# Inverting the RWKV chunk matrices with the transposed factor in the other head's partitions, and the product copied by ScalarE

## The reference, cut to what matters

```python
def rwkv7_scan(r, decay, k, v, a_in, b_in):
    def step(state, inp):
        r_t, w_t, k_t, v_t, a_t, b_t = inp
        sa = jnp.einsum('bhvk,bhk->bhv', state, a_t)
        state = (state * w_t[:, :, None, :] + sa[..., None] * b_t[:, :, None, :]
                 + v_t[..., None] * k_t[:, :, None, :])
        y = jnp.einsum('bhvk,bhk->bhv', state, r_t)
        return state, y
```

## Time and profile before

| | us |
|---|---|
| median of three runs | 2758.38 |
| the profiled execution, its own time | 2757.62 |
| its span, first to last instruction | 2755.8 |
| PE, matmuls busy | 2643.4 |
| DVE (VectorE) busy | 1314.2 |
| ACT (ScalarE) busy | 833.2 |
| POOL (GpSimd) busy | 1038.1 |
| mean granted TensorE clock, of full speed | 0.99 |

### The profile page before, as it was taken

How to read it: one execution, slowest core, us unless ns; L and a number is a source line. 1 busy time by engine, 2 the same in 40 slices (tenths; PEclk the granted TensorE clock), 3 DMA queues, 4 the chain that set the end, 5 groups by cost and what they waited for, 6 DMA issues and landing times.

```text
span 2755.8 us, 43028 instructions
## 1 busy us (share of the span) xinstructions
PE 2643.4 (96%) x17184; PEld 2155.1 (78%) x17184; DVE 1314.2 (48%) x2476; ACT 833.2 (30%) x1687; POOL 1038.1 (38%) x1310
## 2 busy tenths in 40 slices
PE   6999999999999999998899899999999998999999
PEld 5778787877877878776688788788887887877777
DVE  4224343436847567476542533543335006477743
ACT  3344443535224131231213311211113103455531
POOL 2322332333233231320357533344445555444452
PEclk9999999999999999999999999999999999999999
DMA  3111111111101011111332211111111113111122
GB/s 130 40 40 47 50 39 50 47 43 46 44 24 58 21 47 35 37 47 51 150 122 77 84 35 42 46 40 46 46 46 46 46 46 100 35 51 39 47 108 84
DMA packets 203991, 153.94 MB, mean 56 GB/s; under 512 B 5264, under 2 KB 183824, under 8 KB 203280
## 3 DMA queue, kind: packets, MB, share of 16 engines
q1 hardware_dynamic: 186256, 106.44, 13.0%
q10 hardware_dynamic: 17536, 44.74, 4.3%
HBM read 128.10 MB, written 23.07 MB: 55 GB/s over the span
## 4 chain that ended last, share of the span: by engine, by line
PE 76%; DVE 15%; ACT 6%; POOL 2%; issue 1%; DMA 0%; DVEq 0%; ACTq 0%; SPq 0%; POOLq 0%
PE gemm L621 19%; PE gemm L623 18%; PE gemm L622 18%; ACT prob L2382 3%; DVE neg_logits L1807 2%; DVE prob L1822 2%; PE scores L672 1%; PE scores L869 1%; PE weighted L699 1%; PE probs_t L866 1%; PE probs_t L684 1%; PE scores L1046 1%; PE scores L858 1%; DVE stats L1811 1%; PE max_rows L884 1%
## 5 line engine op out<-in xcount | busy, mean ns | idle before, releaser
L582 POOL CAST w_hi<-w_raw 128x512 fp32r<-128x512 f32 x346 | 239.5, 692 | 1597.8 <-PE gemm L623 1531.4
L621 PE MATMUL gemm<-h_hi,w_hi 128*128 128x512 f32 x1904 | 779.1, 409 | 11.0 <-ACT q_t L2024 7.6
L623 PE MATMUL gemm<-h_hi,w_lo 128*128 128x512 f32 x1904 | 747.3, 392 | 0.0
L622 PE MATMUL gemm<-h_lo,w_hi 128*128 128x512 f32 x1904 | 746.1, 392 | 0.0
L584 POOL TENSOR_TENSOR w_lo<-w_raw,w_hi 128x256 fp32r<-128x256 f32 x692 | 590.0, 853 | 54.7
L621 PEld LDWEIGHTS gemm<-h_hi,w_hi 128*128 128x128 f32 x1904 | 360.3, 189 | 91.1 <-issue 22.6
L623 PEld LDWEIGHTS gemm<-h_hi,w_lo 128*128 128x128 f32 x1904 | 359.5, 189 | 78.7
L622 PEld LDWEIGHTS gemm<-h_lo,w_hi 128*128 128x128 f32 x1904 | 360.6, 189 | 66.0 <-issue 1.9
L1589 DVE TENSOR_TENSOR scaled_product<-gemm,norm_rstd 128x512 f32<-128x512 f32 x108 | 74.7, 692 | 310.9 <-PE gemm L623 308.7
L1286 DVE CUSTOM_DVE_ANT_0 neg_logits<-scores,bias_tile 128x128 f32<-128x128 f32 (+1 forms) x192 | 67.6, 352 | 148.7 <-PE scores L672 142.9
L621 PE MATMUL gemm<-xn_hi,w_hi 128*128 128x512 f32 x288 | 117.1, 407 | 4.7 <-DVE xn_lo L1735 4.3
(11 more groups left out here) (512 smaller groups left out, 4541.0 us busy)
## 6 DMA issues: line engine op xcount, KB each, us to landing
w_raw<-in_w_in SPq DMA_DIRECT2D x73, 512.0 KB, 3.9
w_raw<-in_a_w_in SPq DMA_DIRECT2D x48, 512.0 KB, 3.8
gates_scratch<-o_f ACTq DMA_DIRECT2D x32, 256.0 KB, 2.0
merge_gates<-gates_scratch ACTq DMA_DIRECT2D x4, 2048.0 KB, 14.0
w_raw<-in_a_w_out SPq DMA_DIRECT2D x16, 512.0 KB, 3.9
w_raw<-in_b_w_in SPq DMA_DIRECT2D x16, 512.0 KB, 3.8
x_rows<-in_x SPq DMA_DIRECT2D x8, 512.0 KB, 8.6
w_raw<-in_w_out SPq DMA_DIRECT2D x8, 512.0 KB, 4.0
```

The lines of the kernel that those rows point to most:

```text
L582: Q(pool.tensor_copy(weight_part(u, 0, ks), raw[:, s, ks, :]))
L621: pe.matmul(dst, w_high, hi(k, h), start=first, stop=False)
L622: pe.matmul(dst, w_high, lo(k, h), start=False, stop=False)
L623: m = pe.matmul(dst, w_low, hi(k, h), start=False, stop=last)
```

## The change

TT moves into the partitions of the other head, and Tm stays. It is now made like Tm, by TensorE: products with the identity whose input is in one head's partitions and whose output in the other's. The product X = AmT^T Tm also goes from one head's partitions to the other's, into the PSUM banks PV and MB in place of S2. Then X and TT lie side by side, TT^T X leads back to the head's own partitions and X^T TT stays in the other's, and the four products of a chunk number (two heads, two products) name four different quarters; they are issued one after the other. ScalarE copies X to SBUF in place of VectorE. VectorE adds the two halves of Tm first and signals them, then the two halves of TT. TensorE waits for the halves of Tm before X, and for those of TT only before the second products. Its waits for vr_even and vr_odd, which guard PV and MB, now stand before the levels. In AM the first of the three kinds has the heads swapped (L813, L1446, L1464), and in the scan L1507 goes by krows.

```diff
--- before.py
+++ after.py
@@ -810,7 +810,7 @@
                     for i in range(8):
                         for hh, r in enumerate(rows2):
                             c = 8 * cq + i
-                            m = pe.matmul((S2, PT2)[hh][:, i * P:i * P + P], BK[r, c, :, :], AM[r, c, 0:3:2, hh, :], start=True, stop=True)
+                            m = pe.matmul((S2, PT2)[hh][:, i * P:i * P + P], BK[r, c, :, :], AM[r, c].rearrange("p k h t -> p (k h) t")[:, 1 - hh:5 + hh:3 + 2 * hh, :], start=True, stop=True)
                     m.then_inc(E("amat_full"), 1)
 
                 products(0)
@@ -848,31 +848,34 @@
                             m = pe.matmul(PT2[r, c * C:c * C + C], AmT[r, 0, c, :], ident2[r, :], start=True, stop=True)
                     m.then_inc(E("inv_first"), 1)
                     side(p, f"inv{hf}")
+                for hf in range(2):
+                    for r, q in (rows2, rows2[::-1]):
+                        m = pe.matmul(S2[q, halves[hf]], ident2[r, :], AmT[r, 0, 8 * hf:8 * hf + 8, :], start=True, stop=True)
+                    m.then_inc(E("inv_first"), 1)
+                pe.wait_ge(E("vr_even"), 4 * p + 4)
+                pe.wait_ge(E("vr_odd"), 5 * p + 5)
                 for lv in range(1, 6):
-
+                    made = 22 * p + 4 * (lv - 1)
                     pe.wait_ge(E("a_level"), 6 * p + lv + 1)
                     for hf in range(2):
-                        pe.wait_ge(E("inv_sb"), 12 * p + 2 * lv - 1 + hf)
+                        pe.wait_ge(E("inv_sb"), made + 1 + hf)
                         for c in chunk_half[hf]:
-                            for r in rows2:
-                                m = pe.matmul(S2[r, c * C:c * C + C], AmT[r, lv % 2, c, :], Tm[r, c, :], start=True, stop=True)
+                            for r, q in (rows2, rows2[::-1]):
+                                m = pe.matmul((PV, MB)[hf][q, c % 8 * C:c % 8 * C + C], AmT[r, lv % 2, c, :], Tm[r, c, :], start=True, stop=True)
                         m.then_inc(E("invx_full"), 1)
                         side(p, f"inv{4 * lv - 2 + hf}")
                     for hf in range(2):
                         pe.wait_ge(E("invx_sb"), 10 * p + 2 * lv - 1 + hf)
-                        if lv < 5:
-                            for c in chunk_half[hf]:
-                                for r in rows2:
-                                    pe.matmul(PT2[r, c * C:c * C + C], TT[r, c, :], Xs[r, c, :], start=True, stop=True)
+                        pe.wait_ge(E("inv_sb"), made + 3 + hf)
                         for c in chunk_half[hf]:
-                            for r in rows2:
+                            for r, q in (rows2[::-1], rows2):
+                                if lv < 5:
+                                    pe.matmul(PT2[q, c * C:c * C + C], TT[r, c, :], Xs[r, c, :], start=True, stop=True)
                                 m = pe.matmul(S2[r, c * C:c * C + C], Xs[r, c, :], TT[r, c, :], start=True, stop=True)
                         m.then_inc(E("inv_full"), 1)
                         side(p, f"inv{4 * lv + hf}")
 
-                pe.wait_ge(E("vr_even"), 4 * p + 4)
-                pe.wait_ge(E("vr_odd"), 5 * p + 5)
-                pe.wait_ge(E("inv_sb"), 12 * p + 12)
+                pe.wait_ge(E("inv_sb"), 22 * p + 22)
                 for c in range(NCH):
                     n = NCH * p + c
                     pe.wait_ge(E("state"), n + 1)
@@ -1443,7 +1446,7 @@
 
                 for hh, r in enumerate(rows2):
                     V(v.tensor_tensor(AM[r, :, 2, hh, :], chunks(rT[r, :]), chunks(ec[r, :]), ALU.mult))
-                    V(v.scalar_tensor_tensor(AM[r, :, 0, hh, :], chunks(kk[r, :]), -1.0, chunks(logw[r, :]), ALU.mult, ALU.mult))
+                    V(v.scalar_tensor_tensor(AM[r, :, 0, 1 - hh, :], chunks(kk[r, :]), -1.0, chunks(logw[r, :]), ALU.mult, ALU.mult))
                     V(v.tensor_tensor(BK[r, :, hh, :], chunks(kka[r, :]), chunks(cum[r, :]), ALU.mult))
                     V(v.tensor_tensor(BK[r, :, 1 - hh, :], chunks(kmod[r, :]), chunks(cum[r, :]), ALU.mult), E("ak_ready") if hh else None)
                 if p == 0:
@@ -1461,7 +1464,7 @@
                         b, k = rows2[hh], krows[hh]
                         masked(Aab[b, cs, :], bank[b, :, 0, :], mask_a[b, 0:C])
                         masked(AM[b, cs, 1, hh, :], bank[b, :, 1, :], mask_a[b, C:2 * C])
-                        masked(AM[k, cs, 0, hh, :], bank[k, :, 0, :], mask_a[k, 0:C])
+                        masked(AM[k, cs, 0, 1 - hh, :], bank[k, :, 0, :], mask_a[k, 0:C])
                         masked(AM[k, cs, 2, hh, :], bank[k, :, 1, :], mask_a[k, C:2 * C], E("amat_done") if hh else None)
                 for f in range(4):
                     bank = (PV, MB)[f % 2][:].rearrange("p (w x c) -> p w x c", w=4, x=2)
@@ -1474,36 +1477,34 @@
                 def level_of(i):
                     V(v.tensor_tensor(AmT[:, i % 2], Aab[:], level[i].unsqueeze(1).to_broadcast([P, NCH, C]), ALU.mult), E("a_level"))
 
-                eye = ident2.unsqueeze(1).to_broadcast([P, NCH, C])
+                eye = ident2.unsqueeze(1).to_broadcast([P, 8, C])
                 level_of(0)
-                V(v.tensor_tensor(TT[:], AmT[:, 0], eye, ALU.add))
                 level_of(1)
                 ch = [slice(8 * hf, 8 * hf + 8) for hf in range(2)]
                 bank = [slice(HALF * hf, HALF * hf + HALF) for hf in range(2)]
 
-                def rows(ap, hf):
-                    return ap[:, ch[hf]].rearrange("p c t -> p (c t)")
-
-                for hf in range(2):
-                    dve.wait_ge(E("inv_first"), 2 * p + hf + 1)
-                    V(v.tensor_tensor(Tm[:, ch[hf]], PT2[:, bank[hf]].rearrange("p (c t) -> p c t", t=C), ident2.unsqueeze(1).to_broadcast([P, 8, C]), ALU.add), E("inv_sb"))
+                def chunks_of(bank_):
+                    return bank_.rearrange("p (c t) -> p c t", t=C)
+
+                for i, (dst, src) in enumerate(((Tm, PT2), (TT, S2))):
+                    for hf in range(2):
+                        dve.wait_ge(E("inv_first"), 4 * p + 2 * i + hf + 1)
+                        V(v.tensor_tensor(dst[:, ch[hf]], chunks_of(src[:, bank[hf]]), eye, ALU.add), E("inv_sb"))
                 for lv in range(1, 6):
-                    for hf in range(2):
-                        dve.wait_ge(E("invx_full"), 10 * p + 2 * lv - 1 + hf)
-                        V(v.tensor_copy(rows(Xs, hf), S2[:, bank[hf]]), E("invx_sb"))
                     if lv < 5:
                         level_of(lv + 1)
+                        for hf in range(2):
+                            dve.wait_ge(E("inv_full"), 10 * p + 2 * lv - 1 + hf)
+                            V(v.tensor_tensor(Tm[:, ch[hf]], Tm[:, ch[hf]], chunks_of(PT2[:, bank[hf]]), ALU.add), E("inv_sb"))
                     for hf in range(2):
                         dve.wait_ge(E("inv_full"), 10 * p + 2 * lv - 1 + hf)
-                        if lv < 5:
-                            V(v.tensor_tensor(rows(Tm, hf), rows(Tm, hf), PT2[:, bank[hf]], ALU.add))
-                        V(v.tensor_tensor(TT[:, ch[hf]] if lv < 5 else TT2[:, ch[hf], 0, :], TT[:, ch[hf]], S2[:, bank[hf]].rearrange("p (c t) -> p c t", t=C), ALU.add), E("inv_sb"))
+                        V(v.tensor_tensor(TT[:, ch[hf]] if lv < 5 else TT2[:, ch[hf], 0, :], TT[:, ch[hf]], chunks_of(S2[:, bank[hf]]), ALU.add), E("inv_sb"))
                 V(v.memset(SV[lo_, 0, 0, 0, :], 0.0))
                 V(v.memset(SV[hi_, 0, 0, 1, :], 0.0), E("state"))
                 for c in range(NCH):
                     n = NCH * p + c
                     dve.wait_ge(E("sx_full"), n + 1)
-                    for hh, r in enumerate(rows2):
+                    for hh, r in enumerate(krows):
                         V(v.tensor_copy(xs[r, C * hh:C * hh + C], PV[r, C * hh:C * hh + C]), E("sx_sb") if hh else None)
                     for hh, r in enumerate(rows2):
                         V(v.tensor_scalar(se[r, :], SV[r, 0, c, hh, :], e_end[r, c:c + 1], None, ALU.mult))
@@ -2106,8 +2107,12 @@
                     side_out(p, f"rows{f}")
                 for i in range(22):
                     side_out(p, f"inv{i}")
+                for lv in range(1, 6):
+                    for hf in range(2):
+                        act.wait_ge(E("invx_full"), 10 * p + 2 * lv - 1 + hf)
+                        A(a.activation(Xs[:, 8 * hf:8 * hf + 8, :], (PV, MB)[hf][:].rearrange("p (c t) -> p c t", t=C), ACT.Copy), E("invx_sb"))
                 for hf in range(2):
-                    act.wait_ge(E("inv_sb"), 12 * p + 11 + hf)
+                    act.wait_ge(E("inv_sb"), 22 * p + 21 + hf)
                     A(a.activation(TT2[:, 8 * hf:8 * hf + 8, 1, :], TT2[:, 8 * hf:8 * hf + 8, 0, :], ACT.Copy), E("inv_twice"))
                 if p == PAIRS - 1:
                     for k in range(4):
```

## The result

The changed kernel takes 2741.53 us, the median of four runs (2740.52 to 2745.70); the kernel before, 2759.28, the median of four runs (the three named ahead and one more). The ratio is 0.9937, with a 95% interval of 0.9922 to 0.9951. The forecast was a gain of 35.2 us; the two medians are 17.7 apart, half of it. The sign and the range held, the size did not. The profiled execution of the changed kernel is the run of 2745.7 us, with a span of 2743.9, the slowest of the four.

What follows compares the result with a forecast made beforehand. TensorE bounds the whole, but the inverse is a chain where VectorE would set the cycle. 6.76 + 4.36 + 2 x 4.13 + 6.04 = 25.4 us against 34.2, 35.2 us off for four pairs: 2723 us, range 2716 to 2749.

Steps and rivals of the forecast that it cites:

- The start: Inverse from first L848 to the first add of Tm: 6.76 us in place of 7.40.
- The second products: TT^T X and X^T TT in four quarters: 64 records of a half in 0.95 us, before 1.88.
- ScalarE's copies and VectorE's savings: In the inverse, ScalarE copies each half of X in 0.60 us; VectorE loses 7.0 us per pair.
- what costs nothing: Outside the inverse's chain: swapped heads, earlier waits, ScalarE's order, weight ring, DMA and clock should add no time.
- Levels 1 to 4: Inverse cycles between first adds: VectorE sets them, 4.36 us then 4.13 twice; before 6.23, 6.46 and 6.46.
- Level 5 and the end: Inverse from the fourth first add to L879: 6.04 us, before 7.70.
- the 25.4 us: Forecast length of one pair's inverse, L848 to L879, against 34.2 us before.
- Rival (a): Second products: four quarters give no more than two, a half still takes 1.88 us; kernel 2748 us; chance 0.13.
- (b): Second products: quarters sharing rows or columns exclude each other, 3.73 us per half; kernel 2807 us; chance 0.04.
- (c): Inverse: ScalarE's handovers slower (0.5 us: 2730) or a four-quarter half takes 1.3 us (2725); chance 0.10.
- (d): Scans and side work: time goes elsewhere, a weight or result not ready; 2740 if half is lost; chance 0.05.

Runs made afterwards that it cites:

- e1: Changed kernel with half the TensorE instructions in the inverse's levels: each product two chunks wide with the first one's weights, odd chunks wrong; 2721.67 us, ratio 0.9868.
- e3: Changed kernel with the old order of issue: per half all products into PT2, then all into S2, two quarters at a time; 2746.07 us, ratio 0.9955.
- e5: Changed kernel with two quarters at a time and half the instructions in the levels, odd chunks with wrong weights; 2727.15 us, ratio 0.988.
- five steps: Changed kernel with one step of side work (three matmuls) after the second half of X in each inverse level; 2738.81 us, ratio 0.9935.

## Why the prediction was right and wrong

**The start** was right: 6.62 us for 6.76.

**The second products** were right: 15 ns each for the 14.8 of 0.95 us over 64. It was sound to read from two row halves and two column halves that four quarters would be twice as fast as two. The Trainium skill ("TensorE: Matmul & The Clock Gate", Part 3) lets a weight load overlap matmuls only of another row group; the trace does not agree, for in each group of four two pairs share their rows, all four load within 0.02 us, and the next group follows after 0.058 us, hardly more than the 0.053 that 64 columns want by the forecast's reading of the earlier trace rows.

**ScalarE's copies and VectorE's savings** were right: copies 0.60, 6.8 us less on VectorE. So was "what costs nothing": scans within 0.6 us of before, GpSimd at 0.00, clock 1.00, and that with holes of up to 1.7 us where none longer than 0.5 was expected.

**Levels 1 to 4** failed in the sentence "VectorE needs 4.13, so VectorE sets the cycle, and products and copies are hidden by 0.2". It compared VectorE with the chain of products, and left out what TensorE works from. A level has 192 records, 384 instructions, 1.5 packets of 256; at 3.3 to 4.1 us each a level takes 5.0 to 6.1, and 5.03 to 5.59 were measured. This is the mis-sized term: 0.67 + 1.46 + 1.45 us. With fewer instructions (e1) the same sentence is true to 0.01 us.

**Level 5 and the end** was short by 2.03 us for the same reason: 192 records between the last first add and the scan with a hole in them of 1.25, and one of 0.88 (after records 789 and 916).

Both terms are the same over the four pairs: 121.0 - 4 x 25.4 = 19.4 us. Of the 35.2 the inverses gave 136.9 - 121.0 = 15.9.

**Could it have been read?** In part. The page of the kernel before has the same 137 packets for 2 x 17 184 PE instructions, 251 to a packet, and in its four inverses the packets come 3.5 to 5.6 us apart, in pair 0 every 4.3. How fast they come when TensorE asks without pause was not there, so this gave a warning and no bound: 7.56 packets are 26.5 us at the shortest distance and 32.5 at the mean of pair 0, which would have put the kernel between 2727 and 2751 and the 25.4 us in doubt. The prediction counted columns, chains and handovers, and never instructions. It did write that it is wrong "if VectorE pauses in each level", and that is the line that gave it away.

The Trainium skill ("Runtime: NRT & Kernel Launch", Instruction fetch mechanics) speaks of this mechanism: instructions are refilled in blocks of 16 KiB, 256 instructions each, and the cost of going from one block to the next is mostly hidden. The runs agree on the block. They do not agree that it is hidden: it shows here in holes of up to 1.7 us. The same section of the Trainium skill gives TensorE room for 2048 instructions. The trace does not agree that so many lay ready: each hole ended with a packet that had started after the block before the hole, one block of 256 ahead, and the first hole came 276 to 449 records, 552 to 898 instructions, into the inverse.

**Rival (a)** came nearer in time (2748 against 2741.5) than the forecast's 2723, by the wrong mechanism, which is luck, and its price fell with e3 and e5: it assumed that the second batch of products starts when the first is through. **(b)** and **(c)** did not happen. **(d)**, time lost elsewhere, did not either; all of it was lost in the inverse.

**What stays open.** The supply was tested by changing the number of instructions, not the fetch: no run here changes its speed. Why a packet takes 0.9 us at one time and 1.4 at another was not found out. Nor was why five steps are absorbed in pair 0 and only in part in the others, beyond that the packets came 3.5 us apart on average in pair 0 and 3.7 to 4.0 in the others (the first distance of each inverse left out). A kernel that computes every chunk with fewer instructions in the inverse would need products wider than 64 columns with one set of weights; I found none in this algorithm, and none was tried.

## What to carry to other kernels

Beside columns and chains, count TensorE's instructions: here 256 (127 records of small products, their weight loads and two waits) took 3.3 to 4.1 us to arrive in a stretch of 1900, and making products overlap beyond one record in about 29 ns gave little there. The sign in a profile is idle time released by "issue" in the midst of one loop, at a period of 127 records that no loop has. Before costing an overlap in the array, ask what the order does already: here products for idle quarters started ahead of the end of the batch before.

## What was not expected of the hardware

- TensorE stood up to 1.7 us for instructions in the midst of unbroken groups, every 127 records; records resumed some 1.4 us after a packet of 16 384 bytes had ended.
- It had one packet of 256 instructions ahead at most: the packet that ended each of the 21 holes had started 0.9 to 1.7 us after the block before the hole.
- Four records of 64x64 in four quarters start within 0.02 us, and the next four 0.05 to 0.06 later, a rate of 15 ns per record with its weight load.
- Of two batches for different quarters the second starts while six records of the first are still to start (736.36 against 736.53), so that batches of two quarters cost only 1.05 us per inverse more than four interleaved.
- In two quarters a pair of records of 128 columns takes 109 ns to the next pair, where two pairs of 64 columns take 117.
